# Turning block 2's rotated q and k into columns with VectorE block transposes and SBUF transfers in place of TensorE

## The reference, cut to what matters

```python
def hybrid_layer(x, cos, sin, norm_gain, w_in, ..., w_out):
    hn = rms_norm(x, norm_gain)
    proj = jnp.einsum('bsd,de->bse', hn, w_in)          # 3584 columns
    a_q, a_k, a_v, a_g, b_x, b_g, c_q, c_k, c_v, c_g = jnp.split(proj, _in_split_points(), axis=-1)
    qa = apply_partial_rope(a_q.reshape(b, s, 8, 64), cos, sin).transpose(0, 2, 1, 3)   # 8 heads of 64
    ka = apply_partial_rope(a_k.reshape(b, s, 8, 64), cos, sin).transpose(0, 2, 1, 3)
    va = a_v.reshape(b, s, 8, 64).transpose(0, 2, 1, 3)
    y_a = dilated_attention(qa, ka, va).transpose(0, 2, 1, 3).reshape(b, s, 512) * jax.nn.silu(a_g)
    y_b = rg_lru_branch(b_x, ...) * jax.nn.silu(b_g)
    y_c = stick_breaking_attention(...) * jax.nn.silu(c_g)
    return x + jnp.einsum('bse,ed->bsd', jnp.concatenate([y_a, y_b, y_c], axis=-1), w_out)
```

## Time and profile before

| | |
|---|---|
| time before, median of 3 runs | 1153.65 us (1153.38 to 1153.66) |
| the profiled execution's own time | 1153.97 us |
| its span, first to last instruction | 1152.2 us |
| granted TensorE clock, mean | 0.997 |
| TensorE (PE) busy | 1139.4 us, 99% |
| VectorE (DVE) busy | 782.0 us, 68% |
| ScalarE (ACT) busy | 577.5 us, 50% |
| GpSimd (POOL) busy | 96.3 us, 8% |
| read from HBM | 209.37 MB |

### The profile page before, as it was taken

The page is one execution under the profiler, slowest core; times in us unless marked ns, Lnnn a source line. Parts: engine busy times, 40 slices in busy tenths (PEclk is TensorE's granted clock), DMA queues, the critical chain, the costliest instruction groups (busy, mean ns, idle before and its releaser), DMA issues.

```text
span 1152.2 us, 18513 instructions
## 1 busy us (share of the span) xinstructions
PE 1139.4 (99%) x7698; PEld 1036.6 (90%) x7698; DVE 782.0 (68%) x1072; ACT 577.5 (50%) x668; POOL 96.3 (8%) x164
## 2 busy tenths in 40 slices
PE   9999999999999999999999999999999999999997
PEld 7989998998999988989998998899988789878995
DVE  6796868677655456697865867655546766876675
ACT  6555445443444434454545544444443556836673
POOL 0000008201000000000004701000000100010000
PEclk9999999999999999999999999999999999999998
DMA  8754557665756553745456756866566364345420
GB/s 311 269 211 147 174 193 235 219 203 184 240 182 202 174 192 113 253 160 169 158 181 213 241 169 209 265 191 197 161 213 234 105 217 147 131 160 213 147 74 37
DMA packets 134194, 215.81 MB, mean 187 GB/s; under 512 B 8672, under 2 KB 54752, under 8 KB 133984
## 3 DMA queue, kind: packets, MB, share of 16 engines
q1 hardware_dynamic: 128272, 204.15, 52.8%
q0 software_dynamic: 5840, 10.49, 2.9%
HBM read 209.37 MB, written 1.05 MB: 183 GB/s over the span
## 4 chain that ended last, share of the span: by engine, by line
PE 91%; DVE 3%; ACT 3%; issue 1%; DMA 0%; POOL 0%; SPq 0%; POOLq 0%; DVEq 0%; ACTq 0%
PE ps L550 89%; ACT wh L1048 1%; DVE wl L1478 1%; PE ps L707 1%; PE ps L889 0%; ACT L1087 0%; DMA rv<-in_w_in 0%; POOL small L493 0%; ACT L1090 0%; DVE xl L1572 0%; ACT ee L1365 0%; PE ps L871 0%; DVE zz L2049 0%; DVE sg L1787 0%; ACT xh L1084 0%
## 5 line engine op out<-in xcount | busy, mean ns | idle before, releaser
L1478 DVE TENSOR_TENSOR wl<-raw,wh 128x2048 fp32r<-128x2048 f32 (+1 forms) x183 | 410.0, 2246 | 147.9 <-ACT wh L1048 147.6
L1048 ACT ACTIVATE wh<-raw 128x2048 fp32r<-128x2048 f32 x187 | 354.4, 1901 | 185.3 <-PE ps L550 166.5
L550 PE MATMUL ps<-xh,wh 128*128 128x256 f32 x1328 | 370.4, 279 | 0.0
L550 PE MATMUL ps<-xl,wh 128*128 128x256 f32 x1328 | 367.3, 277 | 0.0
L550 PE MATMUL ps<-xh,wl 128*128 128x256 f32 x1312 | 363.5, 277 | 0.0
L550 PEld LDWEIGHTS ps<-xh,wh 128*128 128x128 f32 x1328 | 249.7, 188 | 3.0 <-issue 2.4
L550 PEld LDWEIGHTS ps<-xl,wh 128*128 128x128 f32 x1328 | 249.7, 188 | 0.2
L550 PEld LDWEIGHTS ps<-xh,wl 128*128 128x128 f32 x1312 | 246.8, 188 | 0.0
L550 PE MATMUL ps<-wh,xh 128*128 128x512 f32 (+1 forms) x440 | 169.8, 389 | 1.8 <-DVE xl L1572 1.5
L550 PE MATMUL ps<-wh,xl 128*128 128x512 f32 (+1 forms) x440 | 166.9, 382 | 0.0
L550 PE MATMUL ps<-wl,xh 128*128 128x512 f32 (+1 forms) x440 | 166.7, 382 | 0.0
(11 more groups left out here) (309 smaller groups left out, 1547.3 us busy)
## 6 DMA issues: line engine op xcount, KB each, us to landing
raw<-in_w_in SPq DMA_DIRECT2D x88, 1024.0 KB, 4.9
raw<-in_w_gate_up SPq DMA_DIRECT2D x88, 512.0 KB, 4.7
raw<-in_w_down SPq DMA_DIRECT2D x20, 1024.0 KB, 4.8
raw<-in_w_out SPq DMA_DIRECT2D x16, 1024.0 KB, 4.9
raw<-in_w_proj_ret SPq DMA_DIRECT2D x8, 1024.0 KB, 5.2
raw<-in_w_proj_mlstm SPq DMA_DIRECT2D x8, 1024.0 KB, 5.4
retr<-retb POOLq DMA_DIRECT2D x64, 32.0 KB, 3.1
rows<-in_ln_g POOLq DMA_DIRECT2D x4, 512.0 KB, 4.3
```

Of the source, the lines that this page charges most:

```text
L550: return pe.matmul(o, a, b, start=start, stop=False, skip_group_check=True)
L1048: act.activation(stretch(wh, u, 0, m), source(u)[:, 0:m], ACT.Copy).then_inc(s_hi, 1)
L1478: dve.tensor_tensor(stretch(wl, u, a, nk * n), source(u)[:, a:nk * n], f32(stretch(wh, u, a, nk * n)), ALU.subtract).then_inc(s_lo, 1 if a ...
```

## The change

It touches block 2 alone, once in each of its two layers.

1. TensorE's 16 transposes (`rope_turn`) and the four aux banks that they filled are gone, and with them ScalarE's four copies of 128 x 512.
2. Behind `rope`, VectorE transposes the 32 x 32 blocks of `qk2` into `qkb` (which lies in `sg2`'s memory): two instructions of 128 x 1024, one for each half of the tokens.
3. Sixteen transfers from SBUF to SBUF, each of 32 partitions and 64 KB, carry the blocks to `qkT`, now [128, 2, 4, 256]. GpSimd issues eight (`turn_blocks` 0 and 1), ScalarE eight (2 and 3), in av's slot 2.
4. In av's slot 3, behind the copies of av, ScalarE waits for all 16 and copies q alone into contiguous columns (`qT`, in `qk2`'s memory): four instructions of 128 x 256.
5. TensorE waits for these with `s_qT` in front of the first scores and reads k straight from `qkT`, in pieces of 32 tokens that lie 256 elements apart.

The diff, without the two lines that name the new semaphores and drop `s_rope`:

```diff
-AUX2 = ("r00", "r01", "r10", "r11", "S0", "S1", ...
+AUX2 = ("S0", "S1", ...
-    "av": (("rope",), (), ("turn 0",), ("turn 1",)),
+    "av": (("rope",), (), ("turn",), ("q",)),
...
-            qkT = a4("qkT", [P, 8, S])
+            qkT = a4("qkT", [P, 2, 4, 256])
...
+        qkb = sg2[:, :, :].rearrange("p k t -> p (k t)").rearrange("p (t j x) -> p t j x", t=2, j=4)
+
+        qT = qk2[:, 0, :, :].rearrange("p h d -> p (h d)").rearrange("p (k t) -> p k t", k=4)
+
+        def turn_blocks(eng, i, landed_):
+            for j in range(4):
+                eng.dma_start(qkT[32 * j:32 * j + 32, :, i, :], qkb[32 * i:32 * i + 32, :, j, :]).then_inc(landed_, 16)
...                                                                    # gpsimd
+                pool.wait_ge(s_rflip, l + 1)
+                turn_blocks(pool, 0, s_turnp)
+                turn_blocks(pool, 1, s_turnp)
...                                                                    # tensor
-            def rope_turn(l, c):
-                for t in range(2):
-                    bank, fill = open_aux(f"2r{c}{t}", l)
-                    pe.wait_ge(s_rope, l + 1)
-                    for g in range(4):
-                        in_ = qk2[:, t, 8 * c + 2 * g:8 * c + 2 * g + 2, :].rearrange("p h d -> p (h d)")
-                        r = pe.transpose(bank[:, tok_half(g)], in_, ident)
-                    r.then_inc(fill, 1)
-
             def dil_scores(l, pr):
                 if pr == 0:
-                    for name in ("2r00", "2r01", "2r10", "2r11"):
-                        aux_done(name, l)
+                    pe.wait_ge(s_qT, l + 1)
                 for hh in range(2):
                     bank, fill = open_aux(f"2S{2 * pr + hh}", l)
-                    q_, k_ = qkT[64 * hh:64 * hh + 64, pr, :], qkT[64 * hh:64 * hh + 64, 4 + pr, :]
-                    mm(bank[:, 0:P], q_[:, 0:P], k_[:, 0:P], True)
-                    mm(bank[:, P:P + S], q_[:, P:S], k_[:, :], False).then_inc(fill, 1)
+                    q_ = qT[64 * hh:64 * hh + 64, pr, :]
+                    k_ = qkT[64 * hh:64 * hh + 64, :, :, 128 + 32 * pr:160 + 32 * pr].rearrange("p t i r -> p (t i) r")
+                    mm(bank[:, 0:P], q_[:, 0:P], k_[:, 0:4, :], True)
+                    mm(bank[:, P:P + S], q_[:, P:S], k_, False).then_inc(fill, 1)
...                                                                    # scalar
-            def rope_turn(l, c):
-                for t in range(2):
-                    bank, fill, drained, n = aux(f"2r{c}{t}", l)
-                    act.wait_ge(fill, n + 1)
-                    act.activation(qkT[:, 4 * c:4 * c + 4, tok_half(t)], bank[:, :].rearrange("p (g c) -> p g c", g=4), ACT.Copy).then_inc(drained, 1)
+            def rope_turn(l):
+                act.wait_ge(s_rflip, l + 1)
+                turn_blocks(act, 2, s_turna)
+                turn_blocks(act, 3, s_turna)
+
+            def q_columns(l):
+                act.wait_ge(s_turnp, 128 * (l + 1))
+                act.wait_ge(s_turna, 128 * (l + 1))
+                for k in range(4):
+                    r = act.activation(qT[:, k, :].rearrange("p (n r) -> p n r", r=32),
+                                       qkT[:, :, :, 32 * k:32 * k + 32].rearrange("p t i r -> p (t i) r"), ACT.Copy)
+                r.then_inc(s_qT, 1)
...                                                                    # vector
-                dve.tensor_tensor(x2, q4[2], q4[3], ALU.add).then_inc(s_rope, 1)
+                after(own(dve.tensor_tensor(x2, q4[2], q4[3], ALU.add)))
+                for t in range(2):
+                    r = dve.transpose(qkb[:, t, :, :].rearrange("p j (k r) -> p k j r", k=8),
+                                      qk2[:, t, :, :].rearrange("p h d -> p (h d)").rearrange("p (k j r) -> p k j r", k=8, j=4))
+                r.then_inc(s_rflip, 1)
```

More of the change, by code:

```diff
@@ L150 @@
         "xb00", "xb01", "xb10", "xb11")
-AUX2 = ("r00", "r01", "r10", "r11", "S0", "S1", "S2", "S3", "T0", "T1", "S4", "S5", "V0", "T2", "T3", "S6", "S7", "V1", "T4", "T5",
+AUX2 = ("S0", "S1", "S2", "S3", "T0", "T1", "S4", "S5", "V0", "T2", "T3", "S6", "S7", "V1", "T4", "T5",
         "V2", "c0", "c1", "T6", "T7", "c2", "c3", "V3", "l0", "l1", "k0", "k1", "k2", "k3", "p0", "p1",
@@ L341, in program @@
         s_late = sem("s_late")
-        s_flip, s_low = sem("s_flip"), sem("s_low")
+        s_flip, s_low, s_rflip, s_turnp, s_turna, s_qT = (
+            sem("s_flip"), sem("s_low"), sem("s_rflip"), sem("s_turnp"), sem("s_turna"), sem("s_qT"))
         s_carry = [sem(f"s_carry{n}") for n in range(4)]
@@ L356, in program @@
             sem("s_mixed"), sem("s_mixh"), sem("s_mix"), sem("s_gate"), sem("s_ffm"), sem("s_hidh"), sem("s_hid"), sem("s_hbias"))
-        s_rope, s_den, s_prob, s_silu, s_yraw, s_yh, s_y = (
-            sem("s_rope"), sem("s_den"), sem("s_prob"), sem("s_silu"), sem("s_yraw"), sem("s_yh"), sem("s_y"))
+        s_den, s_prob, s_silu, s_yraw, s_yh, s_y = (
+            sem("s_den"), sem("s_prob"), sem("s_silu"), sem("s_yraw"), sem("s_yh"), sem("s_y"))
         s_ln, s_tail, s_stick, s_conv2, s_lra, s_lre, s_lrv, s_lrs = (
@@ L945, in lru_gates @@
                 r2.then_inc(fill2, 1)
-            steps2 = {"turn": rope_turn, "S": dil_scores, "T": dil_turn, "V": dil_values, "sc": stick_scores, "sk": stick_sums,
+            steps2 = {"S": dil_scores, "T": dil_turn, "V": dil_values, "sc": stick_scores, "sk": stick_sums,
                       "sp": stick_values, "l0": lru_gates}
@@ L1420, in stick_gate @@
                 tanh_half(6, bg)
-            steps = {"turn": rope_turn, "S": dil_exp, "T": dil_turn, "V": dil_out, "ag0": dil_gate, "se": stick_exp, "sl": stick_log,
+            steps = {"turn": rope_turn, "q": q_columns, "S": dil_exp, "T": dil_turn, "V": dil_out, "ag0": dil_gate, "se": stick_exp, "sl": stick_log,
                      "sk": stick_weights, "sp": stick_out, "b0": lru_in, "l0": lru_gates, "l1": lru_decay, "l3": lru_root, "l5": lru_out}
```

## The result

| | before | after |
|---|---|---|
| median time, measured side by side | 1153.52 us (1153.31 to 1153.66, 4 runs) | 1169.39 us (1166.89 to 1170.06, 4 runs) |
| ratio, with its 95% interval | | 1.0134 (1.0123 to 1.0146) |
| profiled execution: own time, span | 1153.97, 1152.2 us | 1169.45, 1167.4 us |
| granted TensorE clock, mean | 0.997 | 0.991 |

What follows compares the result with a forecast made beforehand. TensorE, busy 99% of the span, was taken as the bound. The new path's 15.61 us against rooms of 15.29 and 15.40 gave 0.32 + 0.21 = 0.53 us more: 1154.2 us against the median, range 1151.2 to 1157.6.

Steps and rivals of the forecast that it cites:

- the end of the last issue to the reader's start: Step from GpSimd's last issue to ScalarE's start on the landed data, put at 3.3 us from block 1's 3.02 to 3.66.
- I take 0.4 us: Allowance for the landing being slowed by ScalarE's eight transfers and busy DMA engines, chosen between nothing and 1.3 us.
- What would show it: Listed signs: TensorE waits about 2 us a layer for q's copies; GpSimd's issues take 0.53 us and land last.
- The bound from above: Upper limit for landing delay: block 1's slowest, 5.1 us after issue, so 937.9, 1.3 us later than the 3.3 says.
- ScalarE's transfers are the late ones: Rival: ScalarE's half lands after 937.1, up to 938.8, losing 2.06 and 1.95 us in the layers; 1157.7 us, chance 0.17.
- The clock: Rival: new 2 us waits bring a stretch at 1.2 GHz, costing 4 us, 1158.2 us; chance 0.02.
- the sum: Added steps of the new path from ScalarE's last copy of k to the first scores in layer 0: 15.61 us.
- the flips' 2.37 us: VectorE's two block transposes of 128 x 1024 behind the rotation, put at 2.35 us plus 0.03 for the semaphore.
- the cover: Claim that weight buffers hide VectorE's 2.38 us delay of the next low part; without it, up to 1.8 us a layer.
- k in pieces: TensorE's scores reading k in runs of 32 tokens: taken as nothing; as a rival 4.0 us, 1158.2 us, chance 0.07.
- The end of ScalarE's issues: ScalarE's eight transfer issues, put at 0.42 us each from 930.76, when its second weight split in av ends, to 934.1.
- T: Time of the new path from the start of ScalarE's last copy of k to the first scores; full gain under 13.6 us.

Runs made afterwards that it cites:

- `e10_flips`: The kernel before plus VectorE's two block transposes a layer, whose result nobody reads, and no transfers; 1153.56 us, ratio 1.0001.
- Experiment 1: (`e1_hold`) The changed kernel, with SyncE holding back the weight load that meets the transfers until all 16 have landed; 1152.49 us, ratio 0.999.
- experiment 2: The changed kernel with weight loads held back one load later, so one 1 MB load goes out ahead of the last transfers; 1167.17 us, ratio 1.0109.
- 3: The changed kernel with all sixteen transfers of a layer issued by GpSimd and none by ScalarE; 1171.76 us, ratio 1.0157.
- 4: The changed kernel with transfers of q's blocks alone, 32 KB each instead of 64, scores taken of q with q; 1164.1 us, ratio 1.009.
- experiment 5: The changed kernel with 32 overwritten matmuls of 512 columns in front of TensorE's wait for q's columns; 1165.89 us, ratio 1.0105.
- `e12_diag`: The changed kernel with loads held, four blocks copied by GpSimd, and twelve transfers a layer (GpSimd 2, SyncE 5, ScalarE 5); 1150.93 us, ratio 0.9979.
- `e7_unread_hold`: The kernel before plus block transposes and 16 transfers a layer into unread memory, with SyncE's loads held until they land; 1155.12 us, ratio 1.0012.
- `e4_unread`: The kernel before plus block transposes and 16 transfers a layer into unread memory, without holding loads; 1155.23 us, ratio 1.0015.

## Why the prediction was wrong

**The step that failed** is the landing: "the end of the last issue to the reader's start", 3.3 us, and "I take 0.4 us" for what runs beside. From GpSimd's last issue's end, 932.73, to the copies of q at 942.00 it is 9.27 us in layer 0, 5.57 more than the 3.7. Nor does GpSimd's half land last, as "What would show it" had it: ScalarE's last transfer does, at 941.92. The bound from above, block 1's slowest landing of 5.1 us, was no bound. Block 1's 16 transfers of 32 KB meet two loads of 1 MB as well, but 4.4 to 6.2 us apart, and the DMA engines are busy 54 to 77% of the time meanwhile. Here the two loads are 2.2 us apart (3.85 in the kernel before, at 929.33 and 933.18; VectorE's block transposes push the first one back, since `e10_flips` has the 2.2 us too), twice the bytes are transferred in two thirds of the time, and the engines are busy 92% of 926 to 940. I had the share of 84% in hand and sized its effect by an average over block 1. Experiment 1 shows the cause (the same transfers without the loads: 2.04 us), experiment 2 that a single load is enough, 3 that it isn't ScalarE's queue, 4 that the transfers' own bytes have a smaller part in it. How the DMA engines share out their time, and so why one load is nearly as bad as two, stays open.

**The rival "ScalarE's transfers are the late ones"** had the right place and sign at 0.17, and its price was the same false bound. ScalarE's last transfer is the one on the chain (933.24), and it was issued last. That alone doesn't explain the miss, since GpSimd's last two also took 7.6 us.

**The clock** had 0.02, since the wait was thought to be 2 us. It follows from the first error: waits of 7.2 and 6.3 us were followed by the low clock, and no row shows what 2 us do. It cost 4.4 us, shown by experiment 5.

**The end of the program** wasn't in the sum at all: 1.3 us behind the last instruction, with no row before that could have shown it. That also holds for the best that this change could give: 3.5 us less 1.3 us.

**What was right.** The removed transposes, of whose 3.48 us `e12_diag` gets 3.04 back, and that any wait of TensorE counts in full. The rotation's 3.19 us, the flips' 2.37 (2.35 taken), 0.29 us to GpSimd (0.31), its eight issues in 4.29 (4.25). The block transposes in front of the low parts cost nothing (`e10_flips`), as the cover said. k in pieces costs nothing: 0.93 us for eight records either way. The Trainium skill (SBUF — State Buffer, note on cachelines in the section on the DMA port swizzle) wants two hits on each line of 16 bytes for full speed, which runs of 128 bytes give, and the trace agrees.

**Right by two errors.** The end of ScalarE's issues, 934.1, was right by luck. They were put at 930.76 to 934.1 and took 928.18 to 934.04: they take 0.63 us in the middle case, not 0.42, but begin while ScalarE's split of a weight unit still runs.

**Smaller misses.** ScalarE's four copies of q took 1.33 us, not 1.73. They read in pieces too, at 0.40 us each, so the 498 ns of block 1's row aren't the price of the pieces; whether the scale column or the output's type makes them isn't shown. With the loads held the sum would have erred the other way: in experiment 1 T is 936.49 - 922.32 = 14.17 us, a gain of 1.1 us in layer 0, where the sum had 15.61. From GpSimd's last issue to the copies of q it is then 2.59 us, not 3.7.

## What to carry to other kernels

Before a small transfer on which TensorE waits is put between large loads, find in the trace which load is handed over just before and during it. Landings that were measured with the one or the other alone bound nothing: here the loads alone landed in 4.9 and 5.7 us the transfers with the loads held in 3.3 at most, and together in 9.0 and 10.4 and up to 8.7. A wait in the loading queue that has slack is the cure, and it cost nothing here, where the buffers are far enough ahead (`e7_unread_hold` beside `e4_unread`). A price measured in one stage of the kernel is no bound for another with other traffic. Price each wait of TensorE twice: waits of 4.1 to 7.7 us cost 1.6 to 2.6 us more in lower clock behind them, one of 0.5 us nothing; no run has a wait in between.

## What the runs showed of the hardware that I had not expected

- One load of 1 MB that is handed over in the middle of 16 transfers of 64 KB comes with a last landing that is 3.0 us later in layer 0 and 5.3 us in layer 1 (2.04 and 2.46 us behind the last issue with the loads held, 5.01 and 7.71 with one ahead). At the 402 and 408 GB/s that loads alone reach in 938 to 942 of `e1_hold`, 1 MB would take 2.6 us, an estimate.
- Each transfer between SBUF addresses that GpSimd issues in block 2 lengthens the program by 0.08 us behind its last instruction (6.2 us with none, 8.77 with 32); those of ScalarE and SyncE don't. Why isn't shown.
- The transfers slow the loads as well: 4.9 and 5.7 us to landing without them (`e10_flips`), 9.0 and 10.4 beside them.
- Behind a wait of TensorE of 4.1 to 7.7 us the low clock cost 1.6 to 2.6 us, and the longest waits were among the cheapest (7.6 and 7.7 us, 1.7 and 1.6).
- ScalarE's queue issues transfers while its engine computes: 928.18 beside a split that runs from 928.06 to 929.99.
